# Five first halves of the input projection between the early modulation weights, their second halves in a row

## The chip, the cores and the metric

The kernel runs on one core of a Trainium2 chip. The metric is the device time of one execution in microseconds (us). TensorE (PE) multiplies matrices into eight PSUM banks, ScalarE (ACT), VectorE (DVE) and GpSimd (POOL) work element by element, and SyncE (SP) issues the DMA transfers from HBM.

## The reference

Two layers over 512 tokens (256 of context, 256 of latent), width 2048, all in float32. Only the start of the first layer matters here:

```
shift, scale, gate = split(silu(c) @ ada_w + ada_b, 3)     # "modulation", one set each for context and latent
h  = rms_norm(x, norm_w) * (1 + scale) + shift             # 2048 features = 16 tiles of 128
u, v, ga, q, k, vv, gb = split(h @ w_in, ...)              # "input projection", 44 column tiles of 128
```

`k` and `vv` have two heads of 128 columns, so four column tiles; the rest is worked off in 8 groups of five tiles (q, v, u, ga, gb). A mixer with gating, attention and an output projection follow, then a second layer.

## The kernel before

**Layout.** The normalised input `h` lies in SBUF with the features on the partitions, as 16 feature tiles of 128 x 512 tokens. It is held as a sum of two parts, `hh` (high) and `hl` (low); each weight is split likewise into `wh` and `wl`. A product is three matmuls per feature tile: `hh*wh`, `hl*wh`, `hh*wl` (lines 588 to 590).

**Halves.** The weights of a column tile come as two halves of 512 KB, each for 8 feature tiles. A half is loaded by SP into a slot of the ring, copied to `wh` by ACT (`front_split_hi`, line 345), subtracted to `wl` by POOL (`front_split_lo`, line 350), and used by PE in `front_half` (24 matmuls). ACT, POOL and PE count halves in order of h: h is a half's number in the weight stream. `wh` and `wl` have three buffers: the copy of half h waits until PE has done half h-3 (`front_done`).

**The modulation.** 64 blocks of 512 KB (8 pieces, called eighths here, for each of 8 early blocks) come ahead. PE multiplies each eighth in `ada` (line 551); after an early block ACT copies the result (`ada_rows`, line 1202), PE turns it in `ada_sum` (line 560), DVE adds the bias and, after each second block, prepares the scales (`affine`, line 1633). Each pair of blocks gives shift and scale of four feature tiles: a pass. In a pass DVE scales a feature tile (line 1645), ACT applies scale and shift and writes `hh` (lines 1192, 1195), DVE writes `hl` (line 1657) and raises `h_lo`. The early blocks are numbered 0 to 7 in their order, the passes 0 to 3; pass p needs blocks up to 2p+1.

**Queues.** Every engine works off its own instructions in the written order; what is behind a waiting instruction waits too. The `ada_sum` of block a-1 stands three eighths into block a.

**The ring.** SP loads eighths, halves and later the units for the gate (`w_gate`) and further modulation weights into one ring of 6 slots, in the order of `front_places`. Load n needs the slot of load n-6: it waits until PE has used that eighth (`ada_done`), until POOL has made that half's low part (`front_lo`), or until DVE has read that unit (`unit_done`). Before, halves 0 and 1 are loads 48 and 49 (behind block 5), half 2 is load 58 (behind block 6), halves 3 to 9 are loads 67 to 73, units 0, 1 are 74, 75, halves 10, 11 are 76, 77, units 2, 3 are 78, 79, four late eighths 80 to 83, half 12 is 84.

**Order of the projection before.** PE computes the first half of tile 0 amid block 6 and that of tile 1 amid block 7, their second halves after the last `ada_sum`; the other two k/vv tiles and the first q tile then go as whole tiles. Between them stand the sums for the key norm (line 624), the key rotation (line 630), and two transposes of values (`vv_turn`, line 636). The second of these (`vv_turn(1)`) is reached when PE has done the first five tiles, ten halves.

**The first group.** Behind that point PE does halves 10 and 11, the four late eighths 80 to 83 and a sum over the squares of q (line 683), and then halves 12 and 13. DVE rotates the keys (lines 1700 to 1702) and then works on units 0 to 3, two instructions each (`gate_rows`, line 1686).

Of the kernel before, what the change touches and what calls it, by code (L numbers as in the profile page):

```python
# [14 lines left out]
P = 128  # L15
# [30 lines left out]
SOONER = {5: (0, 1), 6: (2,)}  # L46
# [6 lines left out]
def front_places():  # L53

    place, n = {}, 0

    def half(h):
        nonlocal n
        place["half", h] = n
        n += 1  # L60

    def eighths(a, first, last):
        nonlocal n
        for e in range(first, last):
            place["mod", 8 * a + e] = n
            n += 1

    for a in range(len(EARLY)):
        eighths(a, 0, 8)
        for h in SOONER.get(a, ()):  # L70
            half(h)
    for h in range(3, 4 * KVH):
        half(h)
    for g in range(GROUPS):
        h0, e0 = 4 * KVH + 10 * g, 8 * len(EARLY) + PERGROUP * g
        for t in range(5):
            half(h0 + 2 * t)
            half(h0 + 2 * t + 1)
            if t < 2:
                for u in range(4 * g + 2 * t, 4 * g + 2 * t + 2):  # L80
                    place["unit", u] = n
                    n += 1
            if 1 <= t < 4:
                eighths(0, e0 + 4 * (t - 1), e0 + 4 * t)
    for h in range(4 * KVH + 10 * GROUPS, NHALF0):
        half(h)
    return place
# [36 lines left out]
def build(nc, xT, w_ada, w_gate, cond_row, w_in0, w_out0, w_in1, w_out1, small, mixc, sgu_b, masks, out, keep_x1, keep_g, keep_y):  # L124
    ctx = ExitStack()
    with ctx:
# [196 lines left out]
        OBANK = [0, 1, 3, 4]  # L323

# [88 lines left out]
        def _(sp):  # L413
# [21 lines left out]
            half_loads(w_in0, 0, 3, RING)  # L435
# [4 lines left out]
            half_loads(w_in0, 0, RING, HMIX)  # L440
# [99 lines left out]
        def _(pe):  # L540
# [57 lines left out]

            pe.wait_ge(sem("small_in"), 16)
            pe.wait_ge(sem("consts"), 4)  # L600
            pe.wait_ge(sem("sil_ready"), 1)
            for a in range(NEARLY):
                if a >= 2:
                    pe.wait_ge(sem("mod_added"), a - 1)
                ada(a, 0, 3, pb[2 + a % 2])
                if a:
                    ada_sum(a - 1, pb[2 + (a - 1) % 2])
                if a == 2:
                    square_sum(0)
                ada(a, 3, 5, pb[2 + a % 2])  # L610
                if a >= NEARLY - 2:
                    front_half(a - NEARLY + 2, pb[a - NEARLY + 2][:, :], True, False, "h_lo", 0)
                ada(a, 5, 8, pb[2 + a % 2])
            ada_sum(NEARLY - 1, pb[2 + (NEARLY - 1) % 2])


            KVBANK = [0, 1, 6, 7]

            def kv_tile(n):
                front_tile(2 * n, pb[KVBANK[n]][:, :])  # L620

# [11 lines left out]
            def vv_turn(g):  # L633
                pe.wait_ge(sem("kv_copied"), KVH + g + 1)
                for t in range(NT):
                    done = pe.transpose(pb[5 + g][:, t * P:(t + 1) * P], [a_vT, a_vn][g][:, t * P:(t + 1) * P], ident)
                done.then_inc(sem("vv_turned"), 1)

            ROT = mc[:, MO["rot"][0]:MO["rot"][1]]
            front_half(2, pb[0][:, :], False, True, "h_lo", 1)  # L640
            front_half(3, pb[1][:, :], False, True, None, 1)
            pe.wait_ge(sem("mod_added"), NEARLY)
            k_sum(0)
            kv_tile(2)
            k_sum(1)
            pe.wait_ge(sem("mix_in"), 32)
            k_rotate(0)
            kv_tile(3)
# [18 lines left out]
            for n in range(GROUPS):  # L667
# [3 lines left out]
                front_tile(h, pb[0][:, :])  # L671
                if n:
                    attend(n - 1)
                else:
                    vv_turn(1)
# [6 lines left out]
                pe.wait_ge(sem("q_squared"), n + 1)  # L682
                pe.matmul(pb[3][:, :], ones[:, :], a_sq, start=True, stop=True).then_inc(sem("q_summed"), 1)
# [484 lines left out]
        def _(act):  # L1168
# [53 lines left out]
            for p in range(4):  # L1222
                if p == 2:
                    front_split_hi(act, 0)
                    front_split_hi(act, 1)
                if p == 3:
                    front_split_hi(act, 3)
                act.wait_ge(sem("aff_ready"), p + 1)
                norm_affine(0, 4 * p)
                norm_affine(0, 4 * p + 1)  # L1230
                if p < 3:
                    ada_rows(2 * p + 2, pb[2])
                norm_affine(0, 4 * p + 2)
                norm_affine(0, 4 * p + 3)
                if p == 2:
                    front_split_hi(act, 2)
                if p < 3:
                    ada_rows(2 * p + 3, pb[3])


            def kv_copy(n):
                act.wait_ge(sem("front_done"), n + 3 if n < 2 else 2 * n + 2)
# [16 lines left out]
            front_split_hi(act, 4)  # L1259
            kv_copy(0)  # L1260
            k_square(0)
            front_split_hi(act, 5)
# [3 lines left out]
            front_split_hi(act, 6)  # L1266
            front_split_hi(act, 7)
            kv_copy(2)
            k_root(1)
            front_split_hi(act, HMIX)  # L1270
            front_split_hi(act, HMIX + 1)
# [20 lines left out]
            for n in range(GROUPS):  # L1292
# [5 lines left out]
                else:  # L1298
                    for g in range(KVH):
                        act.wait_ge(sem("vv_turned"), g + 1)  # L1300
                        act.activation(vva[:, g * T:(g + 1) * T], pb[5 + g][:, :], ACT.Copy)\
                           .then_inc(sem("vv_ready"), 1)
# [7 lines left out]
                act.activation(a_q, pb[0][:, :], ACT.Copy).then_inc(sem("q_copied"), 1)  # L1310
                act.activation(a_sq, pb[0][:, :], ACT.Square).then_inc(sem("q_squared"), 1)
# [1076 lines left out]
```

## Time and profile before

| | |
|---|---|
| median of 3 runs | 2515.66 us (2511.03 to 2515.70) |
| profiled execution, own time | 2513.8 us |
| its span in the trace | 2512.0 us |
| PE busy | 2380.4 us, 95% of the span |
| PE busy in 140 to 700 us of the span | 560.0 of 560 us |
| DMA in 20 to 80 us of the span | full, 413 to 415 GB/s |

The span is the time from the first to the last instruction in the trace; 1.8 us lie around it. A row of the timeline begins with its start and its duration; an "idle" in brackets is the time in which that engine had nothing to do just before. Matmuls overlap, so the distance between two starts is the cost of one rather than its duration.

### The profile page before, as it was taken

The page shows a single profiled execution, that of the slowest core. Times are in us where ns is not written, and L with a number is a line of the kernel's source. Part 1 is how long each engine was busy: PE and PEld are TensorE (multiplying, and loading weights), DVE is VectorE, ACT ScalarE, POOL GpSimd, SP SyncE. Part 2 cuts the span into 40 slices and gives each one's busy share as a digit, 9 for nine tenths or more (in the row PEclk, how much of TensorE's full clock was granted, in tenths as well). Part 3 has the DMA queues.
Part 4 walks back from the last instruction along what each step waited for, and adds up shares of the span by engine and source line. Part 5 has one row for each costly group of instructions (what it writes and reads, how often), then busy time and mean ns, then how long its engine had stood idle before and what let it go on. Part 6 is the DMA issues. An engine that isn't in the chain of part 4 may idle for free.

```text
span 2512.0 us, 59174 instructions
## 1 busy us (share of the span) xinstructions
PE 2380.4 (95%) x25844; PEld 1969.6 (78%) x25844; DVE 1132.3 (45%) x2324; ACT 1128.8 (45%) x2025; POOL 1189.6 (47%) x653
## 2 busy tenths in 40 slices
PE   6899999999999968999999999999999999995997
PEld 1377777777778836888888888888888888885997
DVE  1233434433430065555555555555545655553323
ACT  3433333333242245554466446644565446642443
POOL 3133333333345555446654566456644665451554
PEclk9999999999999978999999999999999999998999
DMA  9755655554552123223322332233323332225653
GB/s 401 274 201 176 214 201 214 192 206 177 205 188 92 59 84 105 76 102 102 111 89 91 104 109 87 93 104 102 109 79 103 102 110 78 102 81 198 198 188 118
DMA packets 99490, 353.19 MB, mean 141 GB/s; under 512 B 10784, under 2 KB 15264, under 8 KB 96800
## 3 DMA queue, kind: packets, MB, share of 16 engines
q1 hardware_dynamic: 99232, 349.41, 39.7%
q8 instruction: 204, 3.34, 0.5%
q14 instruction: 54, 0.44, 0.1%
HBM read 337.18 MB, written 12.19 MB: 139 GB/s over the span
## 4 chain that ended last, share of the span: by engine, by line
PE 65%; POOL 16%; DVE 7%; issue 4%; ACT 4%; DMA 3%; SPq 0%; POOLq 0%; DVEq 0%; ACTq 0%
PE bank L588 8%; PE bank L590 8%; PE bank L589 8%; POOL wl L409 7%; PE bank L852 5%; PE bank L746 5%; PE bank L748 4%; PE bank L747 4%; POOL scratch L2201 3%; POOL scratch L2221 3%; PE bank L551 3%; PE bank L1159 2%; PE bank L1161 2%; PE bank L1160 2%; DVE scratch L1837 2%
## 5 line engine op out<-in xcount | busy, mean ns | idle before, releaser
L409 POOL TENSOR_TENSOR wl<-raw,wh 128x1024 fp32r<-128x1024 f32 x214 | 518.3, 2431 | 663.6 <-ACT wh L404 663.6
L746 PE MATMUL bank<-hh,wh 128*128 128x512 f32 (+1 forms) x1040 | 411.0, 395 | 24.3 <-POOL hl L2191 19.6
L588 PE MATMUL bank<-hh,wh 128*128 128x512 f32 x960 | 384.0, 400 | 6.6 <-DVE hl L1657 3.7
L350 POOL TENSOR_TENSOR wl<-raw,wh 128x1024 fp32r<-128x1024 f32 x83 | 203.6, 2464 | 383.2 <-ACT wh L345 383.0
L748 PE MATMUL bank<-hh,wl 128*128 128x512 f32 (+1 forms) x1040 | 383.8, 369 | 0.0
L747 PE MATMUL bank<-hl,wh 128*128 128x512 f32 (+1 forms) x1040 | 382.8, 368 | 0.0
L590 PE MATMUL bank<-hh,wl 128*128 128x512 f32 x960 | 375.1, 391 | 0.0
L589 PE MATMUL bank<-hl,wh 128*128 128x512 f32 x960 | 374.7, 390 | 0.0
L404 ACT ACTIVATE wh<-raw 128x1024 fp32r<-128x1024 f32 x233 | 246.2, 1058 | 268.4 <-PE bank L788 121.8
L746 PEld LDWEIGHTS bank<-hh,wh 128*128 128x128 f32 x1040 | 198.6, 191 | 64.3 <-POOL hl L2191 16.9
L748 PEld LDWEIGHTS bank<-hh,wl 128*128 128x128 f32 x1040 | 198.8, 191 | 34.2
L588 PEld LDWEIGHTS bank<-hh,wh 128*128 128x128 f32 x960 | 180.8, 188 | 56.0 <-POOL wl L350 7.3
L345 ACT ACTIVATE wh<-raw 128x1024 fp32r<-128x1024 f32 x83 | 87.8, 1060 | 294.2 <-DMA raw<-w_in 170.8
L747 PEld LDWEIGHTS bank<-hl,wh 128*128 128x128 f32 x1040 | 199.8, 192 | 25.3
L589 PEld LDWEIGHTS bank<-hl,wh 128*128 128x128 f32 x960 | 181.1, 189 | 38.6 <-issue 2.2
L590 PEld LDWEIGHTS bank<-hh,wl 128*128 128x128 f32 x960 | 180.7, 188 | 38.4
L1837 DVE SCALAR_TENSOR_TENSOR scratch<-bank,sm,scratch 128x508 f32<-128x508 f32 (+3 forms) x256 | 174.1, 680 | 7.5
L786 PE MATMUL bank<-wh,hh 128*128 128x256 f32 x512 | 156.1, 305 | 10.2 <-POOL wl L409 10.2
L350 POOL TENSOR_TENSOR wl<-scratch,wh 128x1024 fp32r<-128x1024 f32 x37 | 90.5, 2457 | 153.1 <-ACT wh L345 153.0
L852 PEld LDWEIGHTS bank<-scratch 32*32 32x32 f32 x10240 | 130.0, 105 | 36.3 <-issue 21.1
L852 PE MATMUL bank<-scratch 32*32 32x64 f32 (+1 forms) x10240 | 143.6, 207 | 12.4 <-DVE scratch L1976 8.1
L788 PE MATMUL bank<-wh,hl 128*128 128x256 f32 x512 | 144.7, 283 | 0.0
(284 smaller groups left out, 4450.4 us busy)
## 6 DMA issues: line engine op xcount, KB each, us to landing
raw<-w_in SPq DMA_DIRECT2D x257, 512.0 KB, 3.5
raw<-w_ada SPq DMA_DIRECT2D x103, 512.0 KB, 5.5
raw<-w_out SPq DMA_DIRECT2D x84, 512.0 KB, 3.7
scratch<-w_ada SPq DMA_DIRECT2D x57, 512.0 KB, 6.0
scratch<-keep_g SPq DMA_DIRECT2D x16, 1024.0 KB, 6.2
scratch<-w_in SPq DMA_DIRECT2D x25, 512.0 KB, 6.8
raw<-w_gate SPq DMA_DIRECT2D x22, 512.0 KB, 4.4
scratch<-xT SPq DMA_DIRECT2D x2, 4096.0 KB, 12.9
```

The source lines that it names most:

```text
L350: eng.tensor_tensor(fl[h % SPLIT], ring[ring_slot("half", h)], fh[h % SPLIT].bitcast(F32), ALU.subtract)\
L404: eng.activation(buffers(s)[0], raw[:, s % RAW, :], ACT.Copy).then_inc(sem("rear_hi"), 1)
L409: eng.tensor_tensor(buffers(s)[1], raw[:, s % RAW, :], buffers(s)[0].bitcast(F32), ALU.subtract)\
L588: pe.matmul(ps, w[:, k * P:(k + 1) * P], hhv[:, kk, :], start=first and k == 0, stop=False)
L589: pe.matmul(ps, w[:, k * P:(k + 1) * P], hlv[:, kk, :], start=False, stop=False)
L590: done = pe.matmul(ps, r[:, k * P:(k + 1) * P], hhv[:, kk, :], start=False, stop=last and k == HALF - 1)
L746: pe.matmul(ps, w[:, k * P:(k + 1) * P], hhv[:, kk, t0:t1], start=first and k == k0, stop=False)
L747: pe.matmul(ps, w[:, k * P:(k + 1) * P], hlv[:, kk, t0:t1], start=False, stop=False)
L748: done = pe.matmul(ps, r[:, k * P:(k + 1) * P], hhv[:, kk, t0:t1], start=False, stop=last and k == k1 - 1)
L786: pe.matmul(ps, hhv[:, k, t0:t0 + P], wk, start=(k == 0 and tt == 0), stop=False)
L852: done = pe.matmul(base_bank[g][bs, m, s0:s1, :], ZC[bs, k, :], DU[bs, k, s0:s1, :], start=True, stop=True)
L1837: ins = dve.scalar_tensor_tensor(out=o3[:, :, a:b], in0=i3[:, :, a + d:b + d], scalar=tap, in1=o3[:, :, a:b], op0=ALU.mult, op1=ALU.add)
```

## The change

Five tiles instead of two get their first halves between the early modulation weights. The weight stream is put in another order: halves 0 to 4 are the first halves of the four k/vv tiles and of the first q tile, halves 5 to 9 their second halves. Half 0 is load 40 now (behind block 4), halves 1 and 2 are loads 49 and 50 (behind block 5), half 3 is load 59 (behind block 6), half 4 is load 68 (behind block 7), and halves 5 to 9 follow as loads 69 to 73; all later places are as before.

PE does first half 0 after block 5, 1 amid block 6, 2 after it, 3 amid block 7, 4 after the last `ada_sum`; then the five second halves, with the key sums and rotation between them. ACT gets the copies at new places: 0 at the end of pass 1, 1 and 2 in the middle of pass 2, 3 at its end, 4 ahead of pass 3, 5 to 7 behind it. The q tile is in bank 5, and the value transposes go into banks 3 and 6. The diff's core:

```
-SOONER = {5: (0, 1), 6: (2,)}
+SOONER = {4: (0,), 5: (1, 2), 6: (3,), 7: (4,)}
...
+        SOONBANK = [0, 1, 6, 7, 5]
+        VVBANK = [3, 6]
...
-            half_loads(w_in0, 0, 3, RING)
+            half_loads(w_in0, 0, 5, HMIX)
...
-            half_loads(w_in0, 0, RING, HMIX)
...
+            def first_half(n):
+                front_half(n, pb[SOONBANK[n]][:, :], True, False, "h_lo", 0)
+
+            def second_half(n, ready=None):
+                front_half(5 + n, pb[SOONBANK[n]][:, :], False, True, ready, 1)
...
-                ada(a, 3, 5, pb[2 + a % 2])
-                if a >= NEARLY - 2:
-                    front_half(a - NEARLY + 2, pb[a - NEARLY + 2][:, :], True, False, "h_lo", 0)
-                ada(a, 5, 8, pb[2 + a % 2])
+                if a == 6:
+                    first_half(1)
+                if a == 7:
+                    first_half(3)
+                ada(a, 3, 8, pb[2 + a % 2])
+                if a == 5:
+                    first_half(0)
+                if a == 6:
+                    first_half(2)
             ada_sum(NEARLY - 1, pb[2 + (NEARLY - 1) % 2])
+            first_half(4)
...
-            front_half(2, pb[0][:, :], False, True, "h_lo", 1)
-            front_half(3, pb[1][:, :], False, True, None, 1)
+            second_half(0, "h_lo")
+            second_half(1)
             pe.wait_ge(sem("mod_added"), NEARLY)
             k_sum(0)
-            kv_tile(2)
+            second_half(2)
             k_sum(1)
+            second_half(3)
             pe.wait_ge(sem("mix_in"), 32)
             k_rotate(0)
-            kv_tile(3)
+            second_half(4)
             k_rotate(1)
             vv_turn(0)
...
             for p in range(4):
-                if p == 2:
-                    front_split_hi(act, 0)
-                    front_split_hi(act, 1)
                 if p == 3:
-                    front_split_hi(act, 3)
+                    front_split_hi(act, 4)
                 act.wait_ge(sem("aff_ready"), p + 1)
                 norm_affine(0, 4 * p)
                 norm_affine(0, 4 * p + 1)
+                if p == 2:
+                    front_split_hi(act, 1)
+                    front_split_hi(act, 2)
                 if p < 3:
                     ada_rows(2 * p + 2, pb[2])
                 norm_affine(0, 4 * p + 2)
                 norm_affine(0, 4 * p + 3)
+                if p == 1:
+                    front_split_hi(act, 0)
                 if p == 2:
-                    front_split_hi(act, 2)
+                    front_split_hi(act, 3)
```

On PE, before, from the end of block 5 into block 6 (L551 is an eighth's matmul, L560 an `ada_sum`, L588 to L590 the projection; banks 2 and 3 are the modulation's): first half 0 stands behind the fifth eighth of block 6.

```order
108 L551 MATMUL bank2<-raw,scratch4 32x512 [waits ring_in2,mod_added]
109 L551 MATMUL bank2<-raw,scratch4 32x512
110 L551 MATMUL bank2<-raw,scratch4 32x512 [waits ring_in3]
111 L551 MATMUL bank2<-raw,scratch4 32x512
112 L551 MATMUL bank2<-scratch2,scratch4 32x512 [waits ring_in4]
113 L551 MATMUL bank2<-scratch2,scratch4 32x512
114 L560 MATMUL bank3<-sm,scratch6 128x2 [waits rows_ready]
115 L560 MATMUL bank3<-sm,scratch6 128x2 x3
116 L551 MATMUL bank2<-scratch3,scratch4 32x512 [waits ring_in5]
117 L551 MATMUL bank2<-scratch3,scratch4 32x512
118 L551 MATMUL bank2<-raw,scratch4 32x512 [waits ring_in0]
119 L551 MATMUL bank2<-raw,scratch4 32x512
```

After the change the same three eighths of block 6 and the same sum are followed at once by first half 1 (lines are 552, 561 and 589 to 591 there):

```order
132 L552 MATMUL bank2<-raw,scratch4 32x512 [waits ring_in3,mod_added]
133 L552 MATMUL bank2<-raw,scratch4 32x512
134 L552 MATMUL bank2<-scratch2,scratch4 32x512 [waits ring_in4]
135 L552 MATMUL bank2<-scratch2,scratch4 32x512
136 L552 MATMUL bank2<-scratch3,scratch4 32x512 [waits ring_in5]
137 L552 MATMUL bank2<-scratch3,scratch4 32x512
138 L561 MATMUL bank3<-sm,scratch6 128x2 [waits rows_ready]
139 L561 MATMUL bank3<-sm,scratch6 128x2 x3
140 L589 MATMUL bank1<-hh,wh 128x512 [waits h_lo,front_lo]
141 L590 MATMUL bank1<-hl,wh 128x512
142 L591 MATMUL bank1<-hh,wl 128x512
```

The half in bank 1, half 1, moved from block 7 to this place; half 0 is now ahead of all these rows.

On ACT, before, pass 2 begins with two copies of halves (L345) ahead of the affine steps (L1192, L1195):

```order
50 L1202 ACTIVATE scratch6<-bank3 128x512 [waits ada_summed,ada_done]
51 L345 ACTIVATE wh<-raw 128x1024 [waits ring_in0]
52 L345 ACTIVATE wh<-raw 128x1024 [waits ring_in1]
53 L1192 ACTIVATE scratch12<-scratch14,mod,affa 128x256 [waits h_lo,n_scaled,aff_ready]
54 L1192 ACTIVATE scratch12<-scratch14,mod,affa 128x256 [waits act_step]
```

After it, one copy stands ahead of the rows of block 5 (L1212), and the next two stand behind two feature tiles of pass 2, of which the first waits for the scales (`aff_ready`):

```order
50 L347 ACTIVATE wh<-scratch2 128x1024 [waits ring_in4]
51 L1212 ACTIVATE scratch6<-bank3 128x512 [waits ada_summed,ada_done]
52 L1202 ACTIVATE scratch12<-scratch14,mod,affa 128x256 [waits h_lo,n_scaled,aff_ready]
53 L1202 ACTIVATE scratch12<-scratch14,mod,affa 128x256 [waits act_step]
54 L1205 ACTIVATE hh<-scratch12 128x512 [waits act_step]
55 L1202 ACTIVATE scratch13<-scratch15,mod,affa 128x256 [waits h_lo,n_scaled]
56 L1202 ACTIVATE scratch13<-scratch15,mod,affa 128x256 [waits act_step]
57 L1205 ACTIVATE hh<-scratch13 128x512 [waits act_step]
58 L347 ACTIVATE wh<-raw 128x1024 [waits ring_in1]
59 L347 ACTIVATE wh<-raw 128x1024 [waits ring_in2]
60 L1212 ACTIVATE scratch5<-bank2 128x512 [waits ada_summed,ada_done]
```

So the copy of half 1 moved from ahead of pass 2 to its middle.

## Rows read from the trace of the kernel before

**Rows 1.** Windows: stretch, length, busy per engine, PE clock, DMA share, GB/s.

```profile
80.00:86.00 6.00, 4.94 (x24) 1.61 (x28) 0.00 (x0) 0.73 (x1) 4.52 (x2) 0.72 0.78 275
88.00:90.00 2.00, 2.00 (x10) 1.65 (x9) 0.97 (x2) 1.94 (x4) 0.00 (x0) 1.00 1.02 408
94.00:98.00 4.00, 2.29 (x16) 0.29 (x8) 0.69 (x1) 3.36 (x6) 0.00 (x0) 1.00 0.80 281
118.00:126.00 8.00, 6.89 (x16) 4.51 (x16) 2.68 (x4) 6.33 (x11) 2.37 (x1) 0.57 0.32 96
140.00:160.00 20.00, 20.00 (x90) 16.23 (x89) 9.54 (x13) 7.24 (x9) 7.16 (x4) 1.00 0.28 86
```

**Rows 2.** Timeline of PE, blocks 5 to 7: start, duration, engine, line, operation, idle before.

```profile
73.90 1.05 PE L551 MATMUL bank<-raw,scratch 128*32 128x512 f32 x4 [0.20 <-DMA raw<-w_ada]
...
81.06 3.09 PE L551 MATMUL bank<-raw,scratch 128*32 128x512 f32 x8 [2.87 <-DMA raw<-w_ada]
...
84.94 1.05 PE L560 MATMUL bank<-sm,scratch 128*128 128x2 f32 x8
...
86.92 0.50 PE L588 MATMUL bank<-hh,wh 128*128 128x512 f32 x1
...
92.59 1.48 PE L551 MATMUL bank<-raw,scratch 128*32 128x512 f32 x10
...
94.45 1.05 PE L551 MATMUL bank<-raw,scratch 128*32 128x512 f32 x4
97.21 1.05 PE L551 MATMUL bank<-raw,scratch 128*32 128x512 f32 x4 [1.71 <-DMA raw<-w_ada]
```

**Rows 3.** Timeline of PE, from the last eighth to the first group.

```profile
108.56 1.05 PE L551 MATMUL bank<-raw,scratch 128*32 128x512 f32 x4 [0.50 <-DMA raw<-w_ada]
110.31 1.05 PE L560 MATMUL bank<-sm,scratch 128*128 128x2 f32 x8 [0.70 <-ACT scratch L1202]
...
130.13 1.02 PE L624 MATMUL bank<-scratch,ones 128*128 128x512 f32 x2
...
165.94 0.60 PE L636 MATMUL bank<-sm,scratch 128*128 128x128 f32 x4
...
179.81 0.79 PE L588 MATMUL bank<-hh,wh 128*128 128x512 f32 x1
```

**Rows 4.** Timeline of ACT, passes 1 to 3.

```profile
70.99 0.63 ACT L1195 ACTIVATE hh<-scratch 128x512 fp32r<-128x512 f32 x1
...
87.09 1.24 ACT L1192 ACTIVATE scratch<-scratch,mod,affa 128x256 f32<-128x256 f32 x2 [6.36 <-DVE scratch L1645]
...
98.62 1.04 ACT L345 ACTIVATE wh<-scratch 128x1024 fp32r<-128x1024 f32 x1
109.66 0.60 ACT L1202 ACTIVATE scratch<-bank 128x512 f32<-128x512 f32 x1 [10.01 <-PE bank L551]
...
114.39 1.23 ACT L1192 ACTIVATE scratch<-scratch,mod,affa 128x256 f32<-128x256 f32 x2 [3.19 <-DVE affa L1633]
...
121.56 1.04 ACT L345 ACTIVATE wh<-raw 128x1024 fp32r<-128x1024 f32 x1
```

**Rows 5.** Timeline of SP, loads 61 and on, 64 and on, 83.

```profile
93.68 1.28 SPq L334 DMA_DIRECT2D raw<-w_ada  x3
102.13 0.80 SPq L334 DMA_DIRECT2D scratch<-w_ada  x2
170.64 0.33 SPq L334 DMA_DIRECT2D scratch<-w_ada  x1
```

**Rows 6.** Timeline of DVE (key rotation, a gate unit), then POOL.

```profile
154.84 0.42 DVE L1700 TENSOR_TENSOR scratch<-bank,scratch 128x256 f32<-128x256 f32 x1 [5.74 <-PE bank L630]
157.71 0.75 DVE L1686 CUSTOM_DVE_ANT_0 raw<-raw,scratch,sm 128x512 f32<-128x512 f32 x1
158.38 2.89 DVE L1686 CUSTOM_DVE_ANT_0 raw<-raw,scratch,sm 128x512 f32<-128x512 f32 x1
157.91 2.81 POOL L350 TENSOR_TENSOR wl<-scratch,wh 128x1024 fp32r<-128x1024 f32 x1 [5.42 <-ACT wh L345]
```

More of the change, by code:

```diff
@@ L71, in front_places @@
             half(h)
-    for h in range(3, 4 * KVH):
+    for h in range(5, 4 * KVH):
         half(h)
@@ L609, in _ @@
                     square_sum(0)
-                ada(a, 3, 5, pb[2 + a % 2])
-                if a >= NEARLY - 2:
-                    front_half(a - NEARLY + 2, pb[a - NEARLY + 2][:, :], True, False, "h_lo", 0)
-                ada(a, 5, 8, pb[2 + a % 2])
+                if a == 6:
[7 more added lines that the diff above has]
+                    first_half(2)
             ada_sum(NEARLY - 1, pb[2 + (NEARLY - 1) % 2])
-            KVBANK = [0, 1, 6, 7]
-            def kv_tile(n):
-                front_tile(2 * n, pb[KVBANK[n]][:, :])
+            first_half(4)
             def k_sum(g):
@@ L634, in vv_turn @@
                 pe.wait_ge(sem("kv_copied"), KVH + g + 1)
+                pe.wait_ge(sem("k_root"), KVH)
                 for t in range(NT):
-                    done = pe.transpose(pb[5 + g][:, t * P:(t + 1) * P], [a_vT, a_vn][g][:, t * P:(t + 1) * P], ident)
+                    done = pe.transpose(pb[VVBANK[g]][:, t * P:(t + 1) * P], [a_vT, a_vn][g][:, t * P:(t + 1) * P], ident)
                 done.then_inc(sem("vv_turned"), 1)
             ROT = mc[:, MO["rot"][0]:MO["rot"][1]]
-            front_half(2, pb[0][:, :], False, True, "h_lo", 1)
-            front_half(3, pb[1][:, :], False, True, None, 1)
+            second_half(0, "h_lo")
+            second_half(1)
             pe.wait_ge(sem("mod_added"), NEARLY)
             k_sum(0)
-            kv_tile(2)
+            second_half(2)
             k_sum(1)
+            second_half(3)
             pe.wait_ge(sem("mix_in"), 32)
             k_rotate(0)
-            kv_tile(3)
+            second_half(4)
             k_rotate(1)
@@ L670, in _ @@
                     pe.wait_ge(sem("ug_ready"), n)
-                front_tile(h, pb[0][:, :])
-                if n:
+                    front_tile(h, pb[0][:, :])
                     attend(n - 1)
@@ L682, in _ @@
                 pe.wait_ge(sem("q_squared"), n + 1)
+                if n == 0:
+                    pe.wait_ge(sem("vv_ready"), 1)
                 pe.matmul(pb[3][:, :], ones[:, :], a_sq, start=True, stop=True).then_inc(sem("q_summed"), 1)
@@ L1241, in kv_copy @@
             def kv_copy(n):
-                act.wait_ge(sem("front_done"), n + 3 if n < 2 else 2 * n + 2)
+                act.wait_ge(sem("front_done"), n + 6)
                 dst = [kTa[:, 0:T], kTa[:, T:2 * T], a_vT, a_vn][n]
@@ L1257, in k_root @@
                    .then_inc(sem("k_root"), 1)
-            front_split_hi(act, 4)
+            front_split_hi(act, 5)
+            front_split_hi(act, 6)
+            front_split_hi(act, 7)
             kv_copy(0)
             k_square(0)
-            front_split_hi(act, 5)
+            front_split_hi(act, 8)
             kv_copy(1)
@@ L1265, in _ @@
             k_square(1)
-            front_split_hi(act, 6)
-            front_split_hi(act, 7)
+            front_split_hi(act, 9)
             kv_copy(2)
             k_root(1)
-            front_split_hi(act, HMIX)
-            front_split_hi(act, HMIX + 1)
             kv_copy(3)
@@ L1300, in _ @@
                         act.wait_ge(sem("vv_turned"), g + 1)
-                        act.activation(vva[:, g * T:(g + 1) * T], pb[5 + g][:, :], ACT.Copy)\
+                        act.activation(vva[:, g * T:(g + 1) * T], pb[VVBANK[g]][:, :], ACT.Copy)\
                            .then_inc(sem("vv_ready"), 1)
@@ L1309, in _ @@
                     act.wait_ge(sem("k_summed"), KVH)
-                act.activation(a_q, pb[0][:, :], ACT.Copy).then_inc(sem("q_copied"), 1)
-                act.activation(a_sq, pb[0][:, :], ACT.Square).then_inc(sem("q_squared"), 1)
+                qbank = pb[0 if n else SOONBANK[4]]
+                act.activation(a_q, qbank[:, :], ACT.Copy).then_inc(sem("q_copied"), 1)
+                act.activation(a_sq, qbank[:, :], ACT.Square).then_inc(sem("q_squared"), 1)
                 front_split_hi(act, h + 4)
@@ L2359 @@
     order0 = [2 * t + b for t in tiles0 for b in range(2)]
-    order0[1:3] = order0[2:0:-1]
+    order0[0:10] = [2 * t + b for b in range(2) for t in tiles0[0:5]]
     h0 = h0[order0]
```

## The prediction

> **What bounds the kernel now.** I read the busy shares first, then windows, then the timeline of each engine between 70 and 180 us. In 140 to 160 us PE is busy without a gap, at full clock [rows 1], and the table of the profile has it so until 700 us; so each microsecond by which PE gets there sooner or later moves the end by one. Ahead of it PE is short of work twice: it waits for loads of modulation weights (2.87 us at 81, 1.71 us at 97 [rows 2]), and after the last `ada_sum` at 110.31 [rows 3] it waits for ACT and DVE, which have yet to normalise the last four feature tiles. The change fills these gaps with first halves. The question is when each first half can start, and what each new wait does to the chain load, PE, ACT, POOL, load. My mark is the second value transpose: PE reaches it at 165.94 [rows 3], with ten halves done; ten halves are done there after the change as well.
>
> **Prices.** From rows: a half on PE is 5.67 us (86.92 to 92.59 [rows 2]). An eighth whose weights are there is 0.46 us (four, 92.59 to 94.45 [rows 2]), and the last ahead of an `ada_sum` 1.0 us. From the start of ACT's copy of a half to the issue of the load that waits for its low part are 3.51 us (98.62 [rows 4] to 102.13 [rows 5]); a second half right behind it is 2.4 us later. A load issued into an empty queue lands 3.53 us later (93.68 [rows 5] to 97.21 [rows 2]), and each further one 1.28 us after that (512 KB at the 408 GB/s of [rows 1]). From `ada_sum` to the first affine step of a pass are 2.15 us (84.94 [rows 2] to 87.09 [rows 4]), in pass 3 4.08 us (110.31 [rows 3] to 114.39 [rows 4]); four feature tiles take ACT 7.17 us (114.39 to 121.56 [rows 4]), two 3.59. From the start of a block's last eighth to its `ada_sum` are 1.75 us (108.56 to 110.31 [rows 3]).
>
> **The clock.** A gap can bring PE down from 2.4 to 1.2 GHz. In 80 to 86 us the mean granted clock is 0.72, so 3.4 us were at the lower level, after a gap of 2.87 us; in 118 to 126 us it is 0.57, so 6.9 us, after a gap and with small waits in between; in 94 to 98 us it stays at 1.00 after a gap of 1.71 [rows 1, 2]. At the lower level PE does half as much, so a 3.4 us stretch costs 1.7 us and the longer one 3.4. I price each gap over 2.5 us with work behind it at 1.7, between 0 and 3.4.
>
> **Part 1: half 0 as load 40.** Loads 40 to 45 come as before, the last at 73.90 [rows 2], and PE has used it at 75.0. Load 46 needs slot 4 back. Before, an eighth gave it back at once. Now it holds half 0, whose copy stands on ACT behind the last feature tile of pass 1 (70.99 [rows 4], next step 0.54 later): copy at 71.5, load 46 issued at 75.0, landed at 78.6; load 48 at 81.1. PE stands idle 3.6 us, ends block 5 at 81.7, and does half 0 to 87.4. The clock falls probably, but the eighths are paced by loads anyway, so only its rest costs: 0.8 us (0 to 2). Half 0 ends at 88.2.
>
> **Part 2: half 1 behind the sum of block 5.** Three eighths later, at 90.1, comes this `ada_sum`. Half 1 is the next item on PE, and its copy stands on ACT behind two feature tiles of pass 2, which wait for just this sum. So PE waits for 2.15 + 3.59 + 3.51 = 9.25 us from the sum's start: half 1 begins at 99.4, after a gap of 8.3 us. Queued behind it are the other five eighths, and SP is held too, since loads 55 and 56 wait for the low parts of halves 1 and 2. With 1.7 us for the clock half 1 ends at 106.7. Loads 55 to 58 land from 102.9 to 107.9 (56 is issued at 101.8, when half 2's low part is made), so the last eighth of block 6 starts at 107.9, and half 2 runs from 108.4 to 114.1.
>
> **Part 3: block 7.** ACT has the rows of block 6 at 109.0 and only then two feature tiles, then the copy of half 3 at 113.1; its low part is there at 116.6. PE does three eighths (loads 60 to 62, landed by 113.4), the sum at 116.0, half 3 from 117.0 to 122.7. Load 65 waits for that low part and lands at 120.1, 67 at 122.7, so the remaining eighths run without a gap and the last starts at 124.5. The last `ada_sum` is at 126.25, where it was at 110.31, with four halves done by then instead of two.
>
> **Part 4: the tail of the norm.** Copy of half 4 at 126.1, PE idle 2.4 us, half 4 from 129.6 to 135.3 (a lower clock here costs nothing, since PE waits again). Pass 3 starts at 126.25 + 4.08, ends 7.17 later at 137.5; the copy of half 5 stands behind it, so second half 0 starts at 137.5 + 3.5 = 141.0. Before, the two second halves after the norm had their weights split already. Halves 6 and 7 come 2.4 us apart and are not late. From 130.13 to 165.94 [rows 3] PE did six halves with key sums, rotations and a transpose; the same with five is 35.81 - 5.67 = 30.14. With 1.7 us for the clock the mark is reached at 172.8 instead of 165.94: +6.9 us.
>
> **Part 5: the first group.** The key rotation of head 1 was 11.8 us ahead of the mark (DVE at 154.84 [rows 6]); now second half 4 is in front of it, and it ends on DVE some 1.1 us behind the mark. DVE's gate units, which were done before the mark, come only then, and their slots are what loads 80, 81 and 84 wait for. Units cost 0.68 per instruction, but DVE's third meets POOL's work on half 11 (POOL's load 83 was released 4.70 us behind the mark [rows 3, 5]), and in the trace such an instruction took 2.89 us instead of 0.75 [rows 6]. So unit 1 is done at mark + 5.95, unit 2 at + 7.3; loads 81, 82, 83 and 84 (half 12) land at + 9.6, 10.9, 12.2 and 13.4. Low part of half 12: + 16.9. PE wants it at 179.81, mark + 13.9 [rows 3]: 3.0 us idle, and 0.8 for the clock (0 or 1.7). The bounds are 0, since the mark's own lateness could give DVE more time than I see, and 5, if POOL blocks a unit twice.
>
> The Trainium skill (SBUF, State Buffer, "Who interferes with whom") says of this pair that a DVE instruction with two SBUF inputs and a GpSimd instruction that reads SBUF exclude each other for a whole instruction, whoever is first. Its rule would give the 5.95 above; were the one slow row chance, unit 1 would be done at + 3.9 and the idle time 0.9, and the sum 2.1 us lower. The trace has the 2.89 us beside POOL's 157.91 row, so I keep it.
>
> **Sum.** 6.9 + 3.8 = +10.7 us, with no matmul added or taken. On the profiled execution's 2513.8 us this gives 2524.5; that execution is 1.9 us under the median of 2515.66, on which it is 2526.4. I say 2525. In this case the bounds of clock and group give 2518 to 2530.
>
> **Rivals.** Faster or slower is told here beyond 0.2%, 5 us, about what a measurement of this kernel can tell from no change.
>
> A, faster: the new halves fill the gaps. If half 0 held no load up (-3.5 us) and half 1 were split in time (-8.3 for the gap, -2.5 for the clocks), the last sum would be at 112.0, second half 0 at 126.7 and the mark at 158.5: -7.5 us, 2506. For it speaks that PE has over 10 us of idle time in 75 to 122 us and that five first halves need only the first eight feature tiles. Against it stands ACT's order, in which the copy of half 1 can't come ahead of the scales of pass 2. It decides where half 1's low part is made before 92 us. 4%.
>
> B, no change: the waits are there but cheap. With the clock at full through all gaps (-4.2) and units in time (-3.8), +2.7 us, 2516.5. The gap without a fall of the clock [rows 1] speaks for it, the lengths of 3.6, 8.3 and 5.7 us against it. 13%.
>
> C, much slower: each gap costs as the worst of the trace does, 3.4 us a stretch at half 1, second half 0 and half 12, 2 at half 0, and the group's idle time is 5: +6.9 + 1.2 + 1.7 + 1.7 + 5 + 3.4, about +20, and half of that excess gives +15 to +20, 2529 to 2534. The Trainium skill (TensorE: Matmul & The Clock Gate, Part 1) says that the point at which the clock comes back differs between runs of one kernel; the two lengths in [rows 1] agree. 15%.
>
> The forecast's own case has 68%. Of it nearly all lies over +5, so slower 80%, same 15%, faster 5%. The range takes in the forecast's case, most of C and the upper part of B: 2517 to 2532.
>
> **What would show it.** In the profile after: load 46 issued near 75 and an idle time of 3 to 4 us on PE in block 5; an idle time of about 8 us ahead of half 1, released by POOL; last `ada_sum` near 126; second half 0 near 141 and waiting for POOL, not for `h_lo`; the mark near 173; a wait ahead of half 12 of some 3 us while SP waits for `unit_done`. If the last `ada_sum` comes before 118, or half 1 starts without a gap, parts 1 and 2 are wrong and A holds; if PE has those gaps and the time is still the old one, my claim that PE's lateness at 140 us is never regained is wrong.

## The result and the profile after

The changed kernel takes 2527.56 us (median of 17 runs, 2524.76 to 2530.79), the one before 2513.97 us in as many runs beside it (2508.92 to 2528.94). The ratio is 1.0053, with a 95% interval of 1.0044 to 1.0063: slower by 13.6 us by the medians, where 10.7 were forecast. The profiled execution took 2528.63 us, its span is 2526.8 us, 14.8 more than before.

PE's timeline after, in the columns of before (line 552 is an eighth's matmul, 561 an `ada_sum`, 589 the first matmul of a feature tile of the projection):

```profile
79.14 3.17 PE L552 MATMUL bank<-scratch 128*32 128x512 f32 x8 [3.88 <-DMA scratch<-w_ada]
...
82.97 0.50 PE L589 MATMUL bank<-hh,wh 128*128 128x512 f32 x1
...
90.48 1.05 PE L561 MATMUL bank<-sm,scratch 128*128 128x2 f32 x8
...
99.89 0.79 PE L589 MATMUL bank<-hh,wh 128*128 128x512 f32 x1 [8.35 <-POOL wl L352]
...
106.89 1.92 PE L552 MATMUL bank<-raw,scratch 128*32 128x512 f32 x16
108.64 1.03 PE L552 MATMUL bank<-scratch 128*32 128x512 f32 x4
109.59 0.50 PE L589 MATMUL bank<-hh,wh 128*128 128x512 f32 x1
...
127.15 1.05 PE L561 MATMUL bank<-sm,scratch 128*128 128x2 f32 x8 [0.70 <-ACT scratch L1212]
130.51 0.80 PE L589 MATMUL bank<-hh,wh 128*128 128x512 f32 x1 [2.31 <-POOL wl L352]
...
141.87 0.80 PE L589 MATMUL bank<-hh,wh 128*128 128x512 f32 x1 [4.22 <-POOL wl L352]
...
174.45 1.04 PE L644 MATMUL bank<-sm,scratch 128*128 128x128 f32 x8
175.24 0.48 PE L589 MATMUL bank<-hh,wh 128*128 128x512 f32 x1
...
191.86 0.77 PE L589 MATMUL bank<-hh,wh 128*128 128x512 f32 x1 [2.56 <-POOL wl L352]
```

Read down, the rows are: block 5 resumed after the late load 46; half 0; the sum of block 5; half 1 after the long gap; the eighths of block 6 and half 2; the last sum, 16.84 us later than the 110.31 of [rows 3]; half 4; second half 0; both value transposes, then half 10; half 12. Before, half 10 started 0.36 us behind the mark:

```profile
166.30 0.47 PE L588 MATMUL bank<-hh,wh 128*128 128x512 f32 x1
```

It is 8.9 us later now, so the mark came at 174.9, and half 12 is 12.05 us later than the 179.81 of [rows 3].

ACT shows why half 1 was late. Its copies (line 347) stand where the code puts them: half 0's behind the last feature tile of pass 1, those of halves 1 and 2 behind two feature tiles of pass 2, which start at 92.63:

```profile
71.40 0.63 ACT L1205 ACTIVATE hh<-scratch 128x512 fp32r<-128x512 f32 x1
71.93 1.04 ACT L347 ACTIVATE wh<-scratch 128x1024 fp32r<-128x1024 f32 x1
...
92.63 1.23 ACT L1202 ACTIVATE scratch<-scratch,mod,affa 128x256 f32<-128x256 f32 x2 [8.94 <-DVE scratch L1657]
...
96.22 1.99 ACT L347 ACTIVATE wh<-raw 128x1024 fp32r<-128x1024 f32 x2
...
138.34 1.04 ACT L347 ACTIVATE wh<-raw 128x1024 fp32r<-128x1024 f32 x1
```

SP shows what the held slots did to the loads (46 and on; 55 and on):

```profile
75.43 0.81 SPq L336 DMA_DIRECT2D scratch<-w_ada  x2
...
99.86 3.13 SPq L336 DMA_DIRECT2D raw<-w_ada  x3
```

PE's clock in four stretches (columns as in [rows 1]; the clock is the third figure from the right). The first three hold the gaps ahead of load 46, half 1 and second half 0, the last that ahead of half 12:

```profile
78.00:84.00 6.00, 4.86 (x16) 1.43 (x17) 0.00 (x0) 0.60 (x1) 0.00 (x0) 0.72 1.02 417
96.00:104.00 8.00, 4.11 (x12) 3.33 (x13) 1.29 (x2) 2.20 (x3) 4.83 (x2) 0.57 0.30 82
140.00:150.00 10.00, 8.13 (x25) 6.46 (x26) 0.00 (x0) 1.27 (x2) 6.48 (x3) 0.66 0.90 333
190.00:196.00 6.00, 4.14 (x12) 3.33 (x13) 2.84 (x1) 3.03 (x4) 4.04 (x2) 0.72 1.01 369
```

DVE in the first group, with the third gate instruction beside POOL's work on half 11 (DVE rows, then the POOL row):

```profile
174.72 0.42 DVE L1712 TENSOR_TENSOR scratch<-bank,scratch 128x256 f32<-128x256 f32 x1 [4.58 <-PE bank L637]
...
177.32 2.88 DVE L1698 CUSTOM_DVE_ANT_0 raw<-raw,scratch,sm 128x512 f32<-128x512 f32 x1
...
180.14 0.74 DVE L1698 CUSTOM_DVE_ANT_0 raw<-raw,scratch,sm 128x512 f32<-128x512 f32 x1
177.19 2.47 POOL L352 TENSOR_TENSOR wl<-scratch,wh 128x1024 fp32r<-128x1024 f32 x1 [2.92 <-ACT wh L347]
```

**Where the 14.8 us of span lie.** 8.9 up to the mark, 3.1 from there to half 12, most of it the wait of 2.56, and 1.1 behind it, where the clock was low: at the last transposes of the first group (line 724 before, 734 after) PE is at 234.99 instead of 221.84, 13.15 us late.

```profile
221.84 0.93 PE L724 MATMUL bank<-sm,scratch 128*128 128x128 f32 x7
```

```profile
234.99 1.04 PE L734 MATMUL bank<-sm,scratch 128*128 128x128 f32 x8
```

It is still 13.1 us late at the first matmul of the output projection (753.99 against 740.90), where both kernels wait for POOL as long:

```profile
740.90 0.50 PE L588 MATMUL bank<-hh,wh 128*128 128x512 f32 x1 [2.66 <-POOL wl L350]
```

```profile
753.99 0.50 PE L589 MATMUL bank<-hh,wh 128*128 128x512 f32 x1 [2.63 <-POOL wl L352]
```

The remaining 1.6 us come right there. Of the two equal gaps only one brought the clock down (the 20 us behind them, before and after):

```profile
741.00:761.00 20.00, 20.00 (x88) 16.53 (x89) 0.88 (x2) 4.37 (x6) 11.58 (x5) 1.00 0.50 166
```

```profile
754.00:774.00 20.00, 20.00 (x81) 16.36 (x82) 0.88 (x2) 4.47 (x6) 9.93 (x5) 0.91 0.50 168
```

At 0.91 over 20 us, some 3.6 us were at the lower level, half of which is lost; from the first matmul of the output projection to the first sum of layer 2 PE takes 157.2 us instead of 155.6. Whether the change has a part in this isn't settled. Of the twelve profiled executions (the two kernels here and the ten runs below) nine have this fall of the clock, with the same 157.2 us; the kernel before, run 9, which is that kernel with one copy moved, and run 5 have 155.6. The length of the gap doesn't sort them: 2.48 us brought the clock down in run 2 and not in run 5. Nothing of layer 2 is slower (the sum at its start, line 578 before, is 14.7 us later, the end 14.8).

### The profile page after: what moved, and what is told of

It is laid out like the page before. It is cut to its first block, busy times and chain, and to the rows that moved or that the text cites. A ratio compares the mean times of both kernels' runs of the same rounds, so it can differ in the third digit from the quotient of the medians.

```text
span 2526.8 us, 59180 instructions
## 1 busy us (share of the span) xinstructions
PE 2385.7 (94%) x25844; PEld 1976.0 (78%) x25844; DVE 1128.4 (45%) x2324; ACT 1128.2 (45%) x2025; POOL 1188.4 (47%) x653
## 4 chain that ended last, share of the span: by engine, by line
PE 65%; POOL 16%; DVE 7%; issue 4%; ACT 4%; DMA 3%; POOLq 0%; SPq 0%; DVEq 0%; ACTq 0%
PE bank L589 8%; PE bank L591 8%; PE bank L590 8%; POOL wl L411 7%; PE bank L862 5%; PE bank L756 5%; PE bank L758 4%; PE bank L757 4%; POOL scratch L2213 3%; POOL scratch L2233 3%; PE bank L552 3%; PE bank L1169 2%; PE bank L1171 2%; PE bank L1170 2%; DVE scratch L1849 2%
## 5 line engine op out<-in xcount | busy, mean ns | idle before, releaser
L590 PE MATMUL bank<-hl,wh 128*128 128x512 f32 x960 | 376.8, 393 | 0.0
L590 PEld LDWEIGHTS bank<-hl,wh 128*128 128x128 f32 x960 | 182.6, 190 | 39.1 <-issue 2.2
L862 PE MATMUL bank<-scratch 32*32 32x64 f32 (+1 forms) x10240 | 143.6, 207 | 11.6 <-DVE scratch L1988 8.1
```

The costliest lines, as they stand in the source:

```text
L590: pe.matmul(ps, w[:, k * P:(k + 1) * P], hlv[:, kk, :], start=False, stop=False)
L862: done = pe.matmul(base_bank[g][bs, m, s0:s1, :], ZC[bs, k, :], DU[bs, k, s0:s1, :], start=True, stop=True)
```

## The experiments

Each ran beside the kernel before. The differences below are taken against the changed kernel's median of 2527.56 us, which was measured in the same way in another job; the kernel before had medians of 2513.97, 2514.18, 2514.05 and 2512.95 us in the four jobs.

**1. Copies of halves 1 and 2 earlier.**

```
                 if p == 2:
+                    front_split_hi(act, 1)
+                    front_split_hi(act, 2)
...
                 act.wait_ge(sem("aff_ready"), p + 1)
                 norm_affine(0, 4 * p)
                 norm_affine(0, 4 * p + 1)
-                if p == 2:
-                    front_split_hi(act, 1)
-                    front_split_hi(act, 2)
```

> The changed kernel, but ACT copies halves 1 and 2 ahead of pass 2 instead of behind its second feature tile. My theory: half 1 then follows the sum of block 5 without the gap of 8.35 us, the clock does not fall there, and loads 55 and 56 are issued before 90 us. The last modulation sum comes at about 117.5 us instead of 127.15, and the time is 9.5 to 10 us below the changed kernel's 2527.6: about 2518. Rival 'loads': the stretch is bound by the ring, and with the gap gone PE waits for modulation weights instead; then the last sum moves by 3 us at most and the time is 2524 or more.

Measured: 2517.77 us (11 runs), ratio to before 1.0011 (1.0002 to 1.0021); 9.8 us less than the changed kernel. PE's rows: the sum of block 5, half 1, the last sum.

```profile
90.72 1.05 PE L561 MATMUL bank<-sm,scratch 128*128 128x2 f32 x8
91.64 0.48 PE L589 MATMUL bank<-hh,wh 128*128 128x512 f32 x1
...
117.55 1.05 PE L561 MATMUL bank<-sm,scratch 128*128 128x2 f32 x8 [0.70 <-ACT scratch L1212]
```

Half 1 has no bracket: it follows at once, and the last sum is 9.6 us earlier. All of the gap was on the path, and the loads did not hold PE up in its place.

**2. Copy of half 0 earlier.**

```
                 if p < 3:
                     ada_rows(2 * p + 2, pb[2])
+                if p == 1:
+                    front_split_hi(act, 0)
...
-                if p == 1:
-                    front_split_hi(act, 0)
```

> The changed kernel, but ACT copies half 0 between the second and third feature tile of pass 1 (3.6 us earlier) instead of behind the fourth. My theory: load 46 is issued near 71.9 us instead of 75.43, PE's idle time of 3.88 us ahead of it goes, the sum of block 5 and all behind it come 3.5 to 4 us sooner: about 2524. Rival 'slack': the wait for load 46 is made up for behind half 1, whose start does not depend on it; then the time stays at 2527.6 within 1 us.

Measured: 2525.89 us (5 runs), ratio 1.0041 (1.0028 to 1.0054); 1.7 us less. The times alone don't tell this from nothing, since the interval overlaps that of the changed kernel (1.0044 to 1.0063); the trace does, and its effect is about half of what I had written.

```profile
76.55 1.05 PE L552 MATMUL bank<-scratch 128*32 128x512 f32 x4 [1.17 <-DMA scratch<-w_ada]
...
80.00 1.05 PE L552 MATMUL bank<-raw,scratch 128*32 128x512 f32 x4 [1.15 <-DMA raw<-w_ada]
80.98 0.50 PE L589 MATMUL bank<-hh,wh 128*128 128x512 f32 x1
...
97.91 0.80 PE L589 MATMUL bank<-hh,wh 128*128 128x512 f32 x1 [8.35 <-POOL wl L352]
```

Load 46 was issued at 71.97, 3.5 us sooner, but landed at 76.55 instead of 79.14, since it now queues behind others, and load 48 came another 1.15 us late. Half 0 started 2.0 us sooner, and so did half 1, behind a gap as long as before. So the rival is out: no wait is made up for. Not all of the 2.0 us lasts, though: in this execution the clock came back later, half 1 took 7.6 us instead of 7.0, and the last sum is 1.4 us sooner (125.72), half 10 1.2 us (174.05).

**3. Copy of half 5 earlier.**

```
                 if p == 3:
                     front_split_hi(act, 4)
+                    front_split_hi(act, 5)
...
-            front_split_hi(act, 5)
             front_split_hi(act, 6)
```

> The changed kernel, but ACT copies half 5 right behind half 4, ahead of pass 3, instead of behind it. My theory: second half 0 starts when half 4 is done, near 136.5 us instead of 141.87, with no fall of the clock, and waits at most for single feature tiles. That is 5.4 us, and 2.6 us of clock: 6 to 8 us, less up to 2 us if POOL's work on half 5 holds up DVE in pass 3: 2520 to 2522. Rival 'norm': PE then waits as long for the last feature tiles (h_lo), and the time falls by less than 2 us.

Measured: 2522.31 us (8 runs), ratio 1.0030 (1.0020 to 1.0040); 5.3 us less, at the edge of the 2520 to 2522 expected. Second half 0 follows half 4 without an idle row, and half 10 starts at 168.98, 6.3 us sooner. POOL's work on half 5 does hold up DVE in pass 3, as was priced: the first two scalings of a feature tile take 3.47 us instead of 1.28:

```profile
131.05 3.47 DVE L1657 TENSOR_TENSOR scratch<-scratch 128x512 f32<-128x512 f32 x2
```

**4. Gate units 0 and 1 ahead of the second key rotation.**

```
                 dve.wait_ge(sem("k_normed"), g + 1)
+                if g:
+                    gate_rows(0)
+                    gate_rows(1)
                 rope(kTa[:, g * T + SEG:(g + 1) * T], "k_rotated", g + 1, "k_ready")
...
-                gate_rows(4 * n)
-                gate_rows(4 * n + 1)
                 if n:
+                    gate_rows(4 * n)
+                    gate_rows(4 * n + 1)
                     b_merge(n - 1)
```

> The changed kernel, but DVE does gate units 0 and 1 ahead of the second key rotation instead of behind it. My theory: loads 80 and 81 are issued before the mark instead of up to 5.5 us behind it, half 12 lands 3 to 4 us earlier, and the wait of 2.56 us ahead of half 12 goes with its low clock: 3 to 4 us, about 2524. Rival: half 12's load (84) waits for unit 2, which is not sooner done than before, so the wait stays and the time stays within 1 us of 2527.6.

Measured: 2523.66 us (5 runs), ratio 1.0037 (1.0024 to 1.0050); 3.9 us less. By the times alone this is barely told from nothing (the changed kernel has 1.0044 to 1.0063). In the trace the wait ahead of half 12 shrinks from 2.56 to 0.55 us, and the clock stays up:

```profile
190.89 0.47 PE L589 MATMUL bank<-hh,wh 128*128 128x512 f32 x1 [0.55 <-POOL wl L352]
```

From half 10 to half 12 PE takes 2.0 us less than in the changed kernel, and from there to the last transposes of the group 1.5 less, 3.5 in all (this execution is 1.0 us late at half 10, from an earlier place). Unit 2, the rival's point, is done 1.6 us earlier relative to half 10; it isn't as early as units 0 and 1 are, which is why some wait remains.

**5. All four.**

> The changed kernel with all four edits of the runs before at once: ACT's copies of halves 0, 1, 2 and 5 earlier, gate units 0 and 1 ahead of the second key rotation. If the four costs are separate links of one chain, they add: -9.8, -1.7, -5.3 and -3.9 us from 2527.6, so 2507, which is 7 us below the kernel before. Rival: the last pass of the norm then sets the time whatever PE has done; the sum of block 7 at about 116 us plus the pass leaves second half 0 at 126 or later, and the four give only some 15 us together: 2512 or more.

Measured: 2504.24 us (7 runs), ratio 0.9966 (0.9953 to 0.9979): 23.3 us less than the changed kernel and 9.8 less than the kernel before. The four alone sum to 20.7, so within the noise they add, and the rival's 15 us are out. Last sum at 114.38, half 10 at 155.71. Whom PE waited for from 60 to 200 us, in us in total, times and the longest, in the changed kernel and in this one:

```profile
PE bank L589 <- POOL wl L352: 17.4, 4, 8.4
PE bank L552 <- DMA scratch<-w_ada: 5.6, 3, 3.9
```

```profile
PE bank L552 <- DMA scratch<-w_ada: 3.3, 4, 1.5
PE bank L589 <- POOL wl L352: 3.2, 2, 2.3
```

14.2 us of waiting for low parts and 2.3 for loads are gone. The last transposes of the first group come 22.7 us sooner (212.32); the 6.2 us beyond these waits I put down to the clock, by subtraction. A further 1.6 us of this execution are the fall of the clock in the output projection, which it doesn't have; that is not the edits' doing as far as shown.

**6. Half 1 later on PE.**

```
                 if a == 6:
-                    first_half(1)
-                if a == 7:
...
                 if a == 6:
+                    first_half(1)
                     first_half(2)
```

> The changed kernel, but PE does half 1 behind the last eighth of block 6 (just ahead of half 2) instead of behind the third; ACT's copies stay. It asks whether the gap of 8.35 us is PE's place in the order or the late copy. My theory, the late copy: PE goes on with the fourth eighth, then waits for load 55, which is issued only when half 1's low part is made, near 99.9 us; the rest of block 6 ends where it ended (109.7), and halves 1 and 2 follow it, so the last modulation sum comes 5 to 6 us later than 127.15: about 2533. Rival, PE's order: with half 1 out of the way PE does block 6 at once, and the time falls by up to 8 us, to 2520.

Measured: 2531.80 us (5 runs), ratio 1.0075 (1.0062 to 1.0089); 4.2 us more, somewhat less than the 5.4 expected. PE now waits in block 6, for load 55:

```profile
104.61 1.92 PE L552 MATMUL bank<-raw,scratch 128*32 128x512 f32 x4 [10.85 <-DMA raw<-w_ada]
```

The last sum is at 133.44, 6.3 us later; half 10 is only 3.8 us later, as the gap ahead of second half 0 is 2.75 us instead of 4.22 and the clock stays up behind it. So the gap was not PE's order. The late copy closed both ways ahead: by the half itself, and by the ring slot that the half held.

**7. Clock kept up ahead of second half 0.** 16 matmuls of `hh` into bank 4, whose content nobody reads.

```
+            for _ in range(16):
+                pe.matmul(pb[4][:, :], hhv[:, 0, 0:P], hhv[:, 0, :], start=True, stop=True)
             second_half(0, "h_lo")
```

> The changed kernel with 16 matmuls of no use (3.7 us at full clock, into bank 4, whose content nobody reads) between half 4 and second half 0, where PE idled 4.22 us. It asks what the lower clock behind this gap costs. My theory: the stretch at 1.2 GHz from 141 to 147 us goes, the way from second half 0 to the mark takes 30.3 us instead of 33.0, and the time falls by 2 to 2.7 us, to 2525. Rival: the clock falls all the same, or the matmuls delay second half 0; then 2527.6 or more.

Measured: 2536.00 us (6 runs), ratio 1.0090 (1.0074 to 1.0106); 8.4 us more, where 2 to 2.7 less were expected. In the stretch itself the theory holds:

```profile
140.00:150.00 10.00, 9.54 (x42) 7.60 (x41) 0.12 (x1) 3.55 (x6) 7.11 (x3) 1.00 0.82 294
...
142.87 0.50 PE L589 MATMUL bank<-hh,wh 128*128 128x512 f32 x1 [0.46 <-POOL wl L352]
...
173.75 0.48 PE L589 MATMUL bank<-hh,wh 128*128 128x512 f32 x1
```

The clock is 1.00 instead of 0.66, and from second half 0 to half 10 are 30.9 us instead of 33.4. But layer 2, from its first sum (908.43) to the end (2528.4), takes 1620.0 us instead of 1615.6; in the ten traces of kernels without added instructions it takes 1612.4 to 1616.1. The profiled execution, 2530.24 us, was the fastest of the six, so it shows only part of the 8.4 us.

**8. Control to 7.** The same 16 matmuls ahead of half 1.

```
                 if a == 6:
+                    for _ in range(16):
+                        pe.matmul(pb[4][:, :], hhv[:, 0, 0:P], hhv[:, 0, :], start=True, stop=True)
                     first_half(1)
```

> The changed kernel with the same 16 useless matmuls, but in the gap of 8.35 us ahead of half 1 instead of the one ahead of second half 0. It is the control to the run in which they kept the clock up: that one gained 2.7 us by 235 us of the span, as said, and then lost 4.5 us and more in layer 2, in idle time of PE that the profile puts to nothing (issue), where the kernel is the same. Theory: 16 more instructions on PE shift the later program, and layer 2 is slower wherever they stand: the mark stays within 1.5 us of the changed kernel's, and the time is 4 to 9 us over 2527.6. Rival: the loss has to do with the clock kept up; then this run is at 2525 to 2528.

Measured: 2540.67 us (4 runs), ratio 1.0101 (1.0087 to 1.0115); 13.1 us more, beyond the 4 to 9 expected. Half 10 starts at 175.93, as in the changed kernel within 0.7 us, while layer 2 takes 1629.3 us (910.54 to 2539.8) instead of 1615.6. The loss is in layer 2 wherever the 16 stand, so it isn't the clock that was kept up. PE's waits there that the profile puts to nothing in it ("issue"), from 920 us on, in the changed kernel and in this one (line 862 is 864 here):

```profile
PE bank L862 <- issue: 3.2, 3, 1.4
```

```profile
PE bank L864 <- issue: 5.9, 5, 2.4
PE bank L760 <- issue: 3.0, 2, 1.9
PE bank L758 <- issue: 2.0, 1, 2.0
PE bank L759 <- issue: 1.7, 2, 1.0
```

These show some 9 of the 13.7 us. One of them, for example:

```profile
1132.14 0.50 PE L758 MATMUL bank<-hh,wh 128*128 128x512 f32 x1 [1.95 <-issue]
```

The traces also hold the DMA packets of 16 KB that the profile counts as "instruction", and these fit. From 920 us on run 8 has eleven such waits of over 0.5 us, run 7 seven, the changed kernel four (15.7, 9.4 and 5.4 us). Each of them, except the one at line 974 (976 in run 8), ends 1.2 to 1.6 us behind the landing of such a packet; with 173 packets in 1600 us, chance would place about 4% of them so. PE most likely waits there for its own instructions, and 16 more of them shift the places at which a new packet is needed. That is read from coinciding times and no run tests it; why a packet comes too late at one place and not at another stays open.

**9. The kernel before with its one late copy moved.**

```
+                if p == 2:
+                    front_split_hi(act, 2)
                 if p < 3:
                     ada_rows(2 * p + 2, pb[2])
                 norm_affine(0, 4 * p + 2)
                 norm_affine(0, 4 * p + 3)
-                if p == 2:
-                    front_split_hi(act, 2)
```

> The kernel before, with one edit: ACT copies half 2 (load 58) in the middle of pass 2, ahead of the rows of block 6, instead of at its end. There load 64 waited for half 2's low part until 102.13 us. If late copies were costing the kernel before as they cost the changed one, load 64 is issued near 95.5 us and PE has its eighths in time; but PE has work in front of them (a half from 101 to 107), so only the end of block 7 moves, by 1 to 1.5 us: 2512.5 to 2513. Rival: the loads were the bound, and all 6 us of it come back: 2508.

Measured: 2512.25 us (11 runs), ratio 0.9995 (0.9986 to 1.0003): 0.7 us, not told from nothing. Load 64 is issued at 96.39 instead of 102.13, and the last sum comes at 108.94 instead of 110.31; 0.9 of these 1.4 us were there already at the sum of block 5 (84.05 instead of 84.94), ahead of the edit's place, so the edit is worth 0.5 where 1 to 1.5 were expected:

```profile
96.39 0.80 SPq L334 DMA_DIRECT2D scratch<-w_ada  x2
```

So the old arrangement had little to gain from earlier copies; what run 5 gains over it comes with the five first halves.

**10. Half 4's copy earlier too.** On top of the four edits:

```
                 if p == 3:
-                    front_split_hi(act, 4)
                     front_split_hi(act, 5)
...
                 if p == 2:
                     front_split_hi(act, 3)
+                    front_split_hi(act, 4)
```

> The kernel with all four edits, in which ACT also copies half 4 ahead of the rows of block 7, while PE is still at block 7. Half 4 then needs no wait after the last modulation sum (2.31 us in the four-edit kernel), and POOL no longer holds up DVE's scales (2.04 us instead of 0.17). I expect 1.5 to 2.3 us from 2504.2: 2502 to 2502.7. Rival: second half 0 waits for the last feature tiles, which POOL's work on half 5 delays all the same; then under 1 us.

Measured: 2501.38 us (6 runs), ratio 0.9945 (0.9932 to 0.9959), the lowest median of all: 2.9 us below run 5, a little over what I expected, though the two intervals touch. Half 4 follows the last sum at once (115.62 after 114.54), second half 0 waits no more than it did, second half 1 now waits 1.01 us for its low part, and half 10 starts at 153.24, 2.5 us sooner than in run 5.

## Why the prediction was right, point by point

**Part 1 held.** Load 46 at 75.43 (75.0), PE idle for 3.88 us (3.6). The clock did fall, and its whole cost came in the eighths, not in half 0: half 0 started at 82.97 instead of 81.7 and then took 5.67 us. "The eighths are paced by loads anyway" was wrong, the sum of the two was right (half 0 ended at 88.64, forecast 88.2). Run 2 shows that this step is worth 1.7 to 2.0 us, not the 3.5 that rival A and the run's expectation gave it: a load that is issued sooner does not land sooner by as much where the queue is full.

**Part 2 held.** From the sum to half 1 are 9.41 us (9.25), of them 8.35 idle (8.3). Runs 1 and 6 show that it is the late copy and that it counts in full.

**Part 3 held.** Half 2 at 109.59 (108.4), half 3 at 118.03 (117.0), last sum at 127.15 (126.25). The 0.9 us are 0.4 from a start already later by that in block 4, and landings half a microsecond later than counted.

**Part 4: the mechanism held, one term was too small.** Second half 0 started at 141.87 (141.0), waiting for POOL and not for `h_lo`. From there to the mark I had counted 30.1 + 1.7 for the clock; it took 33.0, 1.2 more. With the clock up (run 7) the same way takes 2.5 us less, so 0.8 of the 1.2 is clock, and 0.4 is that the way itself is longer than I counted in whole halves. The mean clock of 0.66 over 140 to 150 us is 6.8 us at the lower level, of which some 5.3 had work in them: the longer of the two lengths of [rows 1], where I took the shorter. Which one comes is not decided by the gap: behind 4.02 us at the same place in run 8 it was the shorter one, and half 10 came 32.4 us behind second half 0 instead of 33.4.

**Part 5 held.** Unit 1 was done at mark + 5.9 (5.95), half 12's copy began at mark + 13.3 (13.4), its matmuls at + 17.0 (16.9). The wait and its clock cost 4.2 us (3.8). The 11.8 us between head 1's rotation and the mark are right for PE (154.14); from the DVE row that I named, 154.84, they are 11.1, and nothing in the sum hangs on it. The rule of the Trainium skill (SBUF, State Buffer, "Who interferes with whom") held as a whole block, not as a slowdown: the trace has 2.88 us for the DVE instruction beside POOL's 2.47, after 0.74 for its like, and the sum needed the 2.1 us that it brought.

**Sum.** The miss of 2.5 us at 235 us of the span (13.15 against 10.7) is 0.9 before second half 0, 1.2 behind it (0.8 of it clock), and 0.4 in the group. The 1.6 us in the output projection are one more fall of the clock. No price of mine contained it, since I looked for gaps only where the change is. That the clock terms came out near their middle elsewhere is partly luck: behind the same gap of 8.35 us half 1 took 7.0 us here and 7.2 to 7.6 in runs 2, 3, 4 and 7, against 5.67 at full clock.

**The rivals.** A (gaps filled) was out in this kernel and is real with other copies: runs 5 and 10 are 9.8 us and 11.6 us under the kernel before beside them. B rested on a clock that does not fall at 3.6 to 8.3 us of idle time; it fell every time. C was too dear for halves 0, 1 and 12 (3.4 us of clock at half 1, where 1.3 were lost), and near for second half 0 (3.4, where 2.5 were). The two lengths of [rows 1] that C names beside the skill's sentence stand at two places of one execution; what shows the difference from run to run is half 1, as above.

## What to carry to other kernels

When work is moved forward on one engine, follow each thing that it needs on the engines that prepare it, and see what stands ahead of it in their order: here PE's new first halves were fine, and three copies behind steps that wait for PE itself made it slower. A slot of a shared ring is held until the slowest reader of the load in it is done, so a late preparation stops the loads of others too. Gaps can be priced from one trace by walking through the chain with its own durations. The clock behind them can't be had as closely: equal gaps cost 1.3 to 1.9 us at half 1 and 1.5 to 2.7 at second half 0, so take a range. And look again at the whole trace when instructions were added, not only at the place of the edit.

## What was not expected of the hardware

Equal gaps don't cost equal. Ahead of half 12, gaps of 2.56, 2.63, 2.66 and 2.76 us (the changed kernel, runs 1, 2 and 3) took PE's clock from 2.4 to 1.2 GHz, and gaps of 2.64, 2.74 and 2.76 us (runs 8, 6 and 7) didn't; from half 12 to the last transposes of the group PE then needs 43.1 to 43.2 us in the former and 41.7 in the latter. The Trainium skill (TensorE: Matmul & The Clock Gate, Part 1) says that the point at which the clock comes up varies from run to run, and half 1's 7.0 to 7.6 us behind equal gaps agree. That the fall itself comes or doesn't behind equal gaps is what these traces show.

16 matmuls of no use, 3.8 us long and hidden in idle time, made the kernel 8.4 and 13.1 us slower, by 4.4 and 13.7 us in the profiled layer 2, where not an instruction was changed. The added waits there end 1.2 to 1.6 us behind the landing of packets of instructions, as far as the coinciding times tell.
